# Mixture-of-experts tiles filled by four experts at once, in lanes of 32 tokens

## What is computed

```python
N_EXPERTS = 32; TOP_K = 4; EXPERT_FF = 128; SHARED_FF = 256; ROUTE_SCALE = 2.5
def moe_ffn(h, p):
    t = h.reshape(-1, d)                                   # here 640 tokens of both groups together
    s = sigmoid(t @ p["w_router"])
    _, idx = top_k(s + p["b_router"], TOP_K)
    sel = take_along_axis(s, idx)
    w = sel / sum(sel) * ROUTE_SCALE                       # gate of each of a token's four choices
    hg, hu = t @ w_e_gate[e], t @ w_e_up[e]
    routed = sum over chosen e of (silu(hg) * hu * gate) @ w_e_down[e]
    shared = (silu(t @ w_s_gate) * (t @ w_s_up)) @ w_s_down
    return routed + shared
# x = x + g2 * rmsnorm(moe_ffn(h2), g_post2), and then the next layer's rmsnorm and modulation
```

## Time and profile before

| | before |
|---|---|
| median of 3 runs | 2956.16 us (2955.13 to 2956.25) |
| the profiled execution | 2964.08 us, of which the span 2962.3 us |
| granted TensorE clock, mean | 0.935 |
| TensorE busy with matmuls | 2582.0 us, 87% |
| TensorE busy with weight loads | 1666.3 us, 56% |
| VectorE / ScalarE / GpSimd busy | 33% / 20% / 12% |
| moved by DMA | 452.96 MB, mean 153 GB/s |

### The profile page before, as it was taken

How to read it: one execution, slowest core, us unless ns; L and a number is a source line. 1 busy time by engine, 2 the same in 40 slices (tenths; PEclk the granted TensorE clock), 3 DMA queues, 4 the chain that set the end, 5 groups by cost and what they waited for, 6 DMA issues and landing times. The chain is left out here.

```text
span 2962.3 us, 32617 instructions
## 1 busy us (share of the span) xinstructions
PE 2582.0 (87%) x11924; PEld 1666.3 (56%) x11924; DVE 980.1 (33%) x1955; ACT 605.9 (20%) x1362; POOL 348.0 (12%) x338
## 2 busy tenths in 40 slices
PE   4999969879999989999829998986999998899993
PEld 2445634456457645677615565545656764577771
DVE  1414301463006334222164242136301633522226
ACT  2221100340014012122132121025001401212221
POOL 0005100011001100111220150000200110011113
PEclk8999989999988999999969999989998999999997
DMA  8441086100542030799853101710033103089996
GB/s 307 143 143 36 29 313 245 36 1 29 187 143 48 29 111 36 289 378 380 304 193 123 64 29 36 294 64 1 29 127 95 42 29 118 29 331 379 378 350 219
DMA packets 189030, 452.96 MB, mean 153 GB/s; under 512 B 30732, under 2 KB 52340, under 8 KB 188916
## 3 DMA queue, kind: packets, MB, share of 16 engines
q1 hardware_dynamic: 139668, 306.49, 29.1%
q10 hardware_dynamic: 31968, 82.02, 7.4%
q0 software_dynamic: 17280, 62.92, 5.8%
HBM read 362.00 MB, written 89.39 MB: 152 GB/s over the span
## 5 line engine op out<-in xcount | busy, mean ns | idle before, releaser
L221 PE MATMUL ps<-hT,ring 128*128 128x512 f32 x896 | 414.4, 617 | 13.7 <-PEq L2756 12.4
L2262 PEld LDWEIGHTS ps<-mixT,ring 128*128 128x128 f32 x2496 | 284.5, 192 | 96.9 <-issue 96.9
L2262 PE MATMUL ps<-mixT,ring 128*128 128x128 f32 x2496 | 297.1, 277 | 35.7 <-PE ps L2278 34.0
L221 PEld LDWEIGHTS ps<-hT,ring 128*128 128x128 f32 x896 | 173.2, 198 | 233.3 <-issue 233.1
L230 PE MATMUL ps<-ring,hT 128*128 128x512 f32 x480 | 212.3, 600 | 8.4 <-PEq L1177 7.4
L1215 POOL TENSOR_TENSOR mix_S<-ring 128x512 f32<-128x512 f32 x16 | 25.2, 1577 | 1197.5 <-POOLq L1352 630.3
L2148 PE MATMUL ps<-ring,mixT 128*128 128x512 f32 x320 | 144.0, 611 | 21.6 <-PEq L2756 21.6
L230 PEld LDWEIGHTS ps<-ring,hT 128*128 128x128 f32 x480 | 91.3, 192 | 122.5 <-issue 120.3
L2278 PE MATMUL ps<-ring,ex_hid 128*128 128x512 f32 x304 | 149.5, 614 | 0.0
L1264 PE MATMUL ps<-late,ring 128*128 128x320 f32 x512 | 144.4, 440 | 5.6 <-PEq L1701 2.5
L1264 PEld LDWEIGHTS ps<-late,ring 128*128 128x128 f32 x512 | 98.0, 193 | 49.8 <-issue 10.9
(11 more groups left out here) (404 smaller groups left out, 3605.0 us busy)
## 6 DMA issues: line engine op xcount, KB each, us to landing
ring<-in_w_e_gate SPq DMA_DIRECT2D x78, 512.0 KB
ring<-in_w_e_up SPq DMA_DIRECT2D x78, 512.0 KB
ring<-in_w_e_down SPq DMA_DIRECT2D x78, 512.0 KB
y_rows<-out_gpost ACTq DMA_DIRECT2D x76, 512.0 KB, 6.3
ring<-in_w_in SPq DMA_DIRECT2D x18, 2048.0 KB, 8.4
y_rows<-hT SPq DMA_DIRECT2D x12, 2560.0 KB, 31.1
ring<-in_w_gate SPq DMA_DIRECT2D x12, 2048.0 KB, 9.7
mixT<-in_w_ada ACTq DMA_DIRECT2D x8, 2048.0 KB, 9.4
```

The costliest lines, as they stand in the source:

```text
L221: pe.matmul(lat, wide[:, k, c], hT[:, k, CTX:TOK], start=(k == 0), stop=(k == kt_n - 1))
L2262: ins = pe.matmul(ps[:, 2 + b, g * P:(g + 1) * P], ew[:, k, :], xT[:, b, k, :], start=(k == 0), stop=(k == KT - 1))
```

## The change

- **Experts in lanes.** The experts are ranked by load and grouped four at a time (`GROUPS = 8`). A tile has 128 slots as before, 32 for each of the group's four experts. A group has as many turns of two tiles as its heaviest expert needs for 64 slots a turn. With the loads above the turns are 3, 2, 2, 2, 2, 1, 1, 1 in layer 0 (14 turns, 28 tiles) and 5, 2, 2, 2, 2, 1, 1, 1 in layer 1 (16 turns, 32 tiles). The groups are run in the order heaviest, lightest, second heaviest, second lightest, and so on (`group_at`).
- **Weights stream.** In `up` the stationary operand is 32 tokens (128x32) and the expert's gate and up weights stream as 256 columns; the four experts' matmuls go to four 32-partition strips of one bank. The hidden layer so comes out token-major and must be transposed (`turn_hidden`) and copied (`hidden_out`, ScalarE) before `down`, which is also done in four strips.
- **Weights by group.** All four experts of a group are loaded (6.3 MB) into one of two sets of slots; a set is reloaded when its group is done (`group_done`). TensorE waits for all four experts before a group's first tile.
- **Rows.** Empty slots hold a number out of bounds, and their rows are neither gathered nor scattered. The result is scattered by an indirect DMA from GpSimd's queue (`scatter`), behind the gather of two tiles later, to row choice x 640 + token of `y_rows`. The fill in `stage_da` goes away.
- **Combination.** The rows are read by plain DMAs on SP's queue; the first choice is added by TensorE with a diagonal matrix of gates; ScalarE does all eight pieces of the modulation; the gate's and modulation's rows are loaded in `stage_tail` already.

```diff
-UNROLL = SLOTS
+UNROLL = 2
+LANES = 4
+GRAIN = P // LANES
+GROUPS = NE // LANES
+PER_TURN = UNROLL * GRAIN
+MAX_TURNS = 2 * TOK // PER_TURN + GROUPS
...
@@ stage_da, SP
-            for a in range(0, spare, TILES):
-                n = min(TILES, spare - a)
-                sp.dma_start(cx.y_rows[...], cx.hT[...]).then_inc(sem("rows_filled"), 16)
...
+def group_at(s):
+    return s // 2 if s % 2 == 0 else GROUPS - 1 - s // 2
...
@@ stage_tail, SP
+            if L + 1 < DEPTH:
+                load_mods(cx, sp, L + 1, 0, m.mods, sem("co_mods_in"))
...
-            with sp.Fori(0, count) as i:
-                for n in range(1, UNROLL + 1):
-                    sp.wait_ge(sem("tile_free"), at(n + 1, i))
-                    load(n, i)
+            for s in range(GROUPS):
+                if s == 1:
+                    sp.wait_ge(sem("slots_free"), 2)
+                    sp.wait_ge(sem("rows_stored"), 16 * TILES)
+                if s >= 2:
+                    sp.wait_ge(sem("group_done"), s - 1)
+                for c in range(LANES):
+                    load(s, c)
@@ GpSimd
+            def scatter(n, i):
+                b = n % 2
+                pool.wait_ge(sem("y_low"), at(n + 3, i))
+                pool.wait_ge(sem("y_high"), at(n + 3, i))
+                pool.tensor_copy(goal[:, b:b + 1], m.dest[:, bass.ds(at(n, i), 1)]).then_inc(sem("goal_ready"), 1)
+                pool.wait_ge(sem("goal_ready"), at(n + 1, i))
+                pool.sem_inc(sem("pool_go"), 1)
+                pool.indirect_dma_start(cx.y_rows, bass.IndirectOffsetOnAxis(ap=goal[:, b:b + 1], axis=0), y[:, b, :],
+                                        None, bounds_check=TOP_K * TOK - 1, oob_is_err=False).then_inc(
+                    sem(f"y_stored{b}"), 16)
...
             with pool.Fori(0, count) as i:
                 for n in range(2, UNROLL + 2):
                     gather(n, i)
+                    scatter(n - 2, i)
@@ TensorE, up(n, i, s) and down(n, i, s)
-                for g in range(2):
-                    for k in range(KT):
-                        ins = pe.matmul(ps[:, 2 + b, g * P:(g + 1) * P], ew[:, k, :], xT[:, b, k, :], ...)
+                for k in range(KT):
+                    for c in range(LANES):
+                        rows = slice(c * GRAIN, (c + 1) * GRAIN)
+                        ew = slots[LANES * (s % 2) + c][0].rearrange("p (g k f) -> p g k f", g=2, k=KT)
+                        ins = pe.matmul(ps[rows, 2 + b, 0:2 * P].rearrange("p (g f) -> p g f", g=2), xT[:, b, k, rows],
+                                        ew[:, :, k, :], start=(k == 0), stop=(k == KT - 1))
...
+                pe.transpose(ps[:, 2 + b, 2 * P:3 * P], hid[:, b, :], cx.ident).then_inc(sem("hid_turned"), 1)
...
+                for h in range(2):
+                    for c in range(LANES):
+                        ins = pe.matmul(ps[rows, 4 + 2 * b + h, :], hidT[:, b, rows],
+                                        slots[LANES * (s % 2) + c][1][:, h * SEC:(h + 1) * SEC], start=True, stop=True)
                 ins.then_inc(sem("tile_down"), 1)
-                pe.wait_ge(sem("tile_down"), at(n + 1, i))
-                pe.sem_inc(sem("tile_free"), 1)
...
-            with pe.Fori(0, count) as i:
-                for n in range(1, UNROLL + 1):
-                    turn(n, i)
-                    down(n - 1, i)
-                    up(n, i)
+            for s in range(GROUPS):
+                for c in range(LANES):
+                    pe.wait_ge(sem(f"weights_full{LANES * (s % 2) + c}"), 48 * (s // 2 + 1))
+                last = turns(pe, s)
+                with pe.Fori(first, last) as i:
+                    for n in range(UNROLL):
+                        up(n, i, s)
+                        turn(n + 1, i)
+                        turn_hidden(n, i)
+                        down(n, i, s)
+                first = last
+                pe.wait_ge(sem("tile_down"), last * UNROLL)
+                pe.sem_inc(sem("group_done"), 1)
@@ VectorE, routing (new steps between rank_mm and ids_ready, and one-hot forms in three instructions)
+            step(dve, dve.tensor_tensor(wide, spread(key, 1, NE), spread(key, 2, NE), ALU.is_gt))
+            dve.tensor_reduce(rank, wide, AX.X, ALU.add)
...
+            step(dve, dve.tensor_tensor(wide, spread(seq, 1, NE), spread(seq, 2, NE), ALU.is_lt))
+            step(dve, dve.tensor_tensor(wide, wide, spread(lead, 1, NE), ALU.mult))
+            step(dve, dve.tensor_reduce(begin, wide, AX.X, ALU.add))
...
+            dve.tensor_tensor(place, spread(row, 1, N_CHOICE), spread(inside, 2, P), ALU.is_equal)
+            step(dve, dve.tensor_tensor(where[:, :, :], spread(iota[:, 0:TABLE], 1, N_CHOICE), spread(quad, 2, TABLE),
+                                        ALU.is_equal))
+            dve.tensor_tensor(where[:, :, :], where[:, :, :], spread(place_of, 2, TABLE), ALU.mult)
@@ stage_combine
-                pool.indirect_dma_start(yg[:, n % BUFS, :], None, cx.y_rows.rearrange("n p d -> (n p) d"), ...)
+                    sp.dma_start(yg[:, n % BUFS, :], cx.y_rows[k * TOK + t * P:k * TOK + (t + 1) * P, :])
...
+                for h in range(2):
+                    ins = pe.matmul(ps[:, 2 * (t % 3) + h, :], diag[:, t, :], yg[:, n % BUFS, h * SEC:(h + 1) * SEC],
+                                    start=False, stop=True)
```

More of the change, by code:

```diff
@@ L2134, in _ @@
                     gather(n, i)
+                    scatter(n - 2, i)
+            for b in range(2):
+                pool.wait_ge(sem(f"y_stored{b}"), count * (16 * UNROLL // 2) + 16)
             pool.wait_ge(sem("xg_ready1"), count * (16 * UNROLL // 2) + 16)
@@ L2464, in _ @@
             step(dve, dve.tensor_copy(cnt[:, 0, :], ps[:, 7, TILES * NE:(TILES + 1) * NE]))
-            step(dve, dve.tensor_scalar(cnt[:, 1, :], cnt[:, 0, :], 0.0, None, ALU.is_gt))
-            for n in range(1, TILES):
-                step(dve, dve.scalar_tensor_tensor(out=cnt[:, 1, :], in0=cnt[:, 0, :], scalar=float(n * P),
-                                                   in1=cnt[:, 1, :], op0=ALU.is_gt, op1=ALU.add))
-            step(dve, dve.tensor_tensor_scan(cnt[:, 2, :], cx.ones[:, 0:NE], cnt[:, 1, :], 0.0, ALU.mult, ALU.add))
@@ L2477, in _ @@
-            step(dve, dve.tensor_reduce(ids[:, 0:1], pick[:, 1, 0, :], AX.X, ALU.add))
-            dve.tensor_scalar(ids[:, 1:2], ids[:, 0:1], float(NE - 1), None, ALU.min).then_inc(sem("ids_ready"), 1)
-            step(dve, dve.tensor_scalar(over[:, :, :], pos[:, :, :], float(P), None, ALU.is_ge))
-            for n in range(2, TILES):
-                step(dve, dve.scalar_tensor_tensor(out=over[:, :, :], in0=pos[:, :, :], scalar=float(n * P),
-                                                   in1=over[:, :, :], op0=ALU.is_ge, op1=ALU.add))
@@ new lines, in _ @@
+            n_of, key, rank, group, lane, seq, t_of, lead, begin, tmp = (cnt[:, j, :] for j in range(10))
+            wide = place.rearrange("p n s -> p (n s)")[:, 0:NE * NE].rearrange("p (a b) -> p a b", a=NE)
+            step(dve, dve.scalar_tensor_tensor(out=key, in0=n_of, scalar=float(NE), in1=iota[:, 0:NE], op0=ALU.mult,
+                                               op1=ALU.subtract))
+            step(dve, dve.tensor_tensor(wide, spread(key, 1, NE), spread(key, 2, NE), ALU.is_gt))
+            dve.tensor_reduce(rank, wide, AX.X, ALU.add)
@@ new lines, in _ @@
+            whole(t_of, n_of, 1.0 / PER_TURN, (PER_TURN - 1.0) / (2 * PER_TURN))
+            step(dve, dve.tensor_scalar(t_of, t_of, 1.0, None, ALU.max))
+            whole(group, rank, 1.0 / LANES, -(LANES - 1.0) / (2 * LANES))
+            dve.scalar_tensor_tensor(out=lane, in0=group, scalar=-float(LANES), in1=rank, op0=ALU.mult, op1=ALU.add)
+            dve.tensor_scalar(seq, group, -2.0, 2.0 * GROUPS - 1.0, ALU.mult, ALU.add)
+            step(dve, dve.tensor_scalar(tmp, group, 2.0, None, ALU.mult))
@@ L2501, in _ @@
[L2501 to L2507 removed]
+            whole(spot[:, 0, :, :], chosen[:, :, 0, :], 1.0 / GRAIN, -(GRAIN - 1.0) / (2 * GRAIN))
@@ L2508, in _ @@
             shared(0)
             dve.wait_ge(sem("table_mm"), 1)
-            dve.tensor_copy(m.table[:, :], ps[:, 3, 0:TABLE]).then_inc(sem("table_known"), 1)
+            known = ps[:, 3, 0:TABLE]
+            for b in range(2):
+                dve.tensor_scalar(goal[:, b:b + 1], col, float(TOP_K * TOK + 2 * b), None, ALU.add)
+            dve.tensor_scalar(tab[:, 0, :], known, 0.0, NO_ROW, ALU.is_equal, ALU.mult)
+            step(dve, dve.tensor_scalar(tab[:, 2, :], known, float(TOK), None, ALU.is_gt))
@@ new lines, in _ @@
+            for k in range(2, TOP_K):
+                step(dve, dve.scalar_tensor_tensor(out=tab[:, 2, :], in0=known, scalar=float(k * TOK), in1=tab[:, 2, :],
+                                                   op0=ALU.is_gt, op1=ALU.add))
+            step(dve, dve.scalar_tensor_tensor(out=tab[:, 1, :], in0=known, scalar=-1.0, in1=tab[:, 0, :], op0=ALU.add,
```

(4 more changed lines are left out.)

290 lines of the change are left out of this document (145 added, 145 removed).

## The result

The changed kernel takes 2924.76 us (median of 4 runs, 2918.15 to 2932.43), 0.9902 of the kernel before, with a 95% interval from 0.9878 to 0.9925. That is 29 to 31 us faster; 62 were forecast. The direction and the range held, the size was half.

The account below looks back on a forecast made before the run. The expert loops were taken as TensorE-bound with DMA engines all but full. Terms: loops -33, start +12, fill -22, combination -20, end +1, sum -62 us: 2902 us profiled, 2894 us as median; range 2840 to 2950.

Parts of the forecast that it names:

- The tile: Expert loops: a tile takes 6.95 us on TensorE, as before, with a 0.4 us gap before down for ScalarE's copy.
- pairs of instructions can't be fed: Rival for up in the expert loops: 107 ns a pair makes a tile 10.35 us, +148, 3042 us; chance 0.09.
- Six waits for weights: Expert loops: TensorE idles 7 to 8 us before the third, fifth and seventh group, granted clock near 0.5 after.
- The combination of layer 1: Start of adding moves 5.5 us earlier and five instructions go, 6.4, less 1 for late rows: -11 us.
- The fill: Layer 0, line 273: without it TensorE's waits of 11.42 and 9.28 us for weights go; -22 us, bounds 0 and -26.
- The loops: Both expert loops: 16 tiles fewer, 111 us, mostly lost to weight waits and low clock, leaving -33 us.
- The start: Start of the expert loop: +4.7 us of VectorE work and +1 at the lower clock, +6 a layer, +12 us.
- The combination: Combination in both layers: rows loaded ahead, ScalarE pacing layer 0's tiles; -9 and -11, -20 us together.
- The end: End of the expert loop: last result scattered by GpSimd instead of stored, mostly in place of the extra up; +1 us.
- GpSimd's pace: Rival: one queue for gather and scatter makes a tile 7.6 us, +31, 2925 us; chance 0.18.
- Weights early: Rival for the expert loops: the three waits fall to 1 or 2 us, clock holds; -50, 2845 us; chance 0.12.
- Fill no hindrance: Rival: the fill did not delay the kernel before, so removing it gains nothing; 2916 us; chance 0.09.

Follow-up runs that it names:

- shared_first: Changed kernel with the shared expert's second half put ahead of the first tile's copies on ScalarE and VectorE: 2920.46 us, 0.9883 of the kernel before.
- turns_between: Changed kernel with TensorE's transpose of tile t-3 placed behind the sum of tile t in the combination: 2916.34 us, 0.9866 of the kernel before.
- fill_back: Changed kernel with the fill put back where it was, into a tensor nobody reads: 2953.25 us, 1.0003 of the kernel before.
- fill_moved: Kernel before, with its fill issued behind the stores of keys and values instead of ahead of the loads: 2931.26 us, 0.9935 of the kernel before.
- no_down_loads: Changed kernel without the down weights' loads of the third to eighth group, old ones used instead: 2882.1 us, 0.9746 of the kernel before.

## Why the prediction was wrong

**Right.** The tile: 6.88 us for 6.95, 60 tiles, the gap before down, strips that run at once. The rival that pairs of instructions can't be fed is refuted: 64 records in 3.57 us, 56 ns each. The Trainium skill's 62 ns for every matmul with the hardware decoder off ("TensorE: Matmul & The Clock Gate", the step on decode and dispatch) would have made it 3.97; the rows here are below it, so it does not bind this kernel. Six waits for weights at the third, fifth and seventh groups, with a clock of 0.50 behind. The combination of layer 1, -10.3 for -11. The fill: -26 for -22, and -29 over the runs; the term was sized without the products behind the waits, which also ran at the lower level, though the bound of -26 had them.

**The loops, -33 against -14.** This is the largest miss: the waits for weights by group. The mechanism was right and the size was off. (1) From one heavy group's end to the next heavy start I took 23.5 us; it was 25.6, 26.6, 25.1, 25.1, 27.2, 26.6, on average 26.0, six times 2.5: 15 us. I took 2.2 for issue, first bytes and landing and 15.0 + 5.1 for the bytes at 409 to 421 GB/s. From the end of the down product to SP's first DMA it is 0.9 alone, and windows at the start of the load have 299, 397 and 362 GB/s, not 415:

```profile
1231.00:1236.00 5.00, 4.79 (x73) 3.35 (x73) 0.47 (x2) 0.34 (x2) 2.28 (x3) 1.00 0.86 299
1236.00:1241.00 5.00, 4.74 (x72) 2.35 (x76) 1.21 (x2) 1.30 (x3) 0.85 (x2) 1.00 1.01 397
1241.00:1246.00 5.00, 3.16 (x35) 1.51 (x29) 0.98 (x2) 1.04 (x3) 1.61 (x3) 1.00 0.98 362
```

The rule of the Trainium skill that I weighed ("DMA: Bandwidth & Descriptors", Specifications, about 358 GB/s as a core's HBM limit) does not describe these windows either: the two after them have 421 and 417. (2) In each first group a turn waits for its gather behind the second group's weights, 2.2 and 1.9 us: 4. I had put no such wait. (3) The low clock cost 11.8 us behind the six waits, where I had 15, and 4.7 more in the two loops' first tiles, where I had none. (4) Tiles were 0.07 us shorter, -4 us. Together that is 17 of the 19 us.

**The start, +12 against +20.** The VectorE part was right: the table's products come 3.4 and 5.3 us later (4.7 forecast). What I had at 1 us a layer was 6.0 and 5.0. I had not looked at what stands behind the first tile's copies on ScalarE and VectorE: the shared half, for which the first up waits. The gather, later now, holds both. shared_first gives back 3.6 to 4.5 us in the stage, 6 by the ratio.

**The combination, -20 against -10.** The step that failed is layer 0, -9. Its sums did start 9 us after the stage did (8 forecast, though the sum's own 1481 is 10 after the stage's start), but I counted ScalarE as the pace and gave TensorE's order no look. Rows by DMA made TensorE's sums wait for transfers for the first time, so everything behind them in its queue waits for them too. By turns_between that is 8.2 us in the stage, most of the 9.6 that were missed; 2.5 more lay in the rows issued behind a store.

**The end, +1 against +4.5.** I had counted the last scatter's issue and nothing behind it. No run was made for it, so this is read from the traces alone. The copies end at 1425.2, the scatter is issued by 1427.5, and its rows have landed by 1428.7; then GpSimd's drain, the instruction that ends the stage on it, lasts until 1433.7, and the next stage starts at 1434.0. The drain in the two layers (shortest, median and longest in ns, first and last start):

```profile
L2018 POOLq DRAIN x2: 4959/5288/5617, 1428.7 to 2861.4; - x2
```

In the kernel before it took 3.2 and 3.5 us, but from 1459.6 and 2886.3 on, beside TensorE's extra up, so nobody waited for it. With the scatter on GpSimd it stands last. What it waits for stays open.

**The rivals.** GpSimd's pace: gathers cost 14.6 us of waits, mostly while weights load and not by the cycle of scatter and gather, which would slow every tile: TensorE waits for a gather 10 times in 60 tiles. No run was made for it alone. Weights early: refuted by the six waits. Fill no hindrance: refuted by fill_back.

What stays open: why neighbourhood attention starts at the lower clock for 17 to 51 us in layer 0, differently in each execution; and what of the 19 to 25 us of fill_moved is lost again later in the kernel.

## What to carry to other kernels

Put each part of a large change back by itself before you credit it: here the fill of 16.8 MB a layer, a side job that the change merely made unnecessary, carried all of the gain, and moving it in the old kernel had most of it. When buffers are freed by the group, what counts is how long the group between runs; sort so that short groups stand at the ends, and price the load from the end of the last reader to the first product, latency included. When an operand of an engine that works in order comes by DMA for the first time, read what is queued behind that instruction on each engine, since that is what the wait costs.

## What was not expected of the hardware

After 8.6 to 10.8 us without a matmul, up ran at 1.2 GHz for 1.3 to 2.8 us of loss, and after waits of 2.4 to 5.1 us in no_down_loads it did in four of six cases; with products going on through the whole wait, none of the six did (3.66 us). A stage of small, dense products (neighbourhood attention, TensorE busy 47.8 of 51.2 us) stayed at 1.2 GHz for 51 us in three of the profiles; in the changed kernel's own it was 20.5 us, and the stretch behind it went on at 1.00. No run here says why. GpSimd's drain at the end of the expert loop's stage took 5.0 and 5.6 us although its last scatter had landed.
